# Three attention units in flight, and four gate products of branch C around the norm of branch A

## The reference

```
# block 1, mixing part (per layer)
y_mla = causal_mla_attention(...) @ w_o_mla          # 8 heads, 96 wide
y_hg  = hgrn2_branch(...) @ w_o_hg
y_mem = memory_branch(...) @ w_o_mem                 # 4 heads, 128 wide
merged = gates[0] * y_mla + gates[1] * y_hg + gates[2] * y_mem
x = x + merged @ w_out

# block 2, mixing part (per layer)
ya = diff_attention(...)        # A: 4 heads, softmax(q0 k0) - lam * softmax(q1 k1), then an rms norm
yb = nsa_attention(...)         # B: 8 heads, three softmaxes each (compressed, selected, window)
yc = swa_sink_attention(...)    # C: 8 heads, window of 128 with a sink
merged = sigmoid(ga) * (ya @ w_branch[0]) + sigmoid(gb) * (yb @ w_branch[1]) + sigmoid(gc) * (yc @ w_branch[2])
h = h + merged @ w_out
```

## Time and profile before

| | before |
|---|---|
| median of three runs | 3007.83 us |
| lowest and highest | 3001.94 and 3012.53 us |
| the profiled execution's own time | 3003.04 us |
| its span | 3001.3 us |
| mean granted TensorE clock | 0.983 of full |
| TensorE matmuls busy | 2910.9 us, 97% |
| TensorE weight loads busy | 2741.8 us, 91% |
| VectorE busy | 1695.5 us, 56% |
| ScalarE busy | 1188.8 us, 40% |
| DMA | 474.41 MB, mean 158 GB/s |

### The profile page before, as it was taken

The page is one execution under the profiler, slowest core; times in us unless marked ns, Lnnn a source line. Parts: engine busy times, 40 slices in busy tenths (PEclk is TensorE's granted clock), DMA queues, the critical chain, the costliest instruction groups (busy, mean ns, idle before and its releaser), DMA issues.

```text
span 3001.3 us, 49531 instructions
## 1 busy us (share of the span) xinstructions
PE 2910.9 (97%) x21376; PEld 2741.8 (91%) x21376; DVE 1695.5 (56%) x2824; ACT 1188.8 (40%) x1771; POOL 12.6 (0%) x20
## 2 busy tenths in 40 slices
PE   8999999999998999999999998999989999899998
PEld 8998788999998878899999996789989999678998
DVE  5666543665666553466666444456656654454665
ACT  5535422444445432244444233234454432332444
POOL 0000000000000000000000000000000000000000
PEclk9999999999999999999999898999999999999999
DMA  7544385555544344455664642445545565234553
GB/s 246 177 152 123 111 205 168 169 179 186 183 158 148 100 140 154 154 183 176 193 200 155 184 129 71 108 163 183 182 156 183 172 181 143 85 99 148 183 182 110
DMA packets 481273, 474.41 MB, mean 158 GB/s; under 512 B 47104, under 2 KB 464416, under 8 KB 480928
## 3 DMA queue, kind: packets, MB, share of 16 engines
q1 hardware_dynamic: 477472, 460.75, 49.2%
q0 software_dynamic: 3584, 10.49, 1.6%
HBM read 464.91 MB, written 6.29 MB: 157 GB/s over the span
## 4 chain that ended last, share of the span: by engine, by line
PE 92%; DVE 4%; ACT 3%; issue 1%; DMA 0%; DVEq 0%; ACTq 0%; SPq 0%
PE ps L829 33%; PE ps L928 32%; PE ps L949 17%; PE ps L982 4%; PE ps L1052 2%; PE ps L1022 1%; DVE WL L1676 1%; ACT WH L1349 1%; PE ps L872 1%; PE ps L876 1%; PE ps L880 1%; ACT REGION L1318 0%; PE ps L860 0%; DVE REGION L1819 0%; ACT L1335 0%
## 5 line engine op out<-in xcount | busy, mean ns | idle before, releaser
L1676 DVE TENSOR_TENSOR WL<-RAW,WH 128x2048 fp32r<-128x2048 f32 (+1 forms) x350 | 780.5, 2235 | 483.7 <-ACT WH L1349 481.6
L1349 ACT ACTIVATE WH<-RAW 128x2048 fp32r<-128x2048 f32 (+1 forms) x350 | 647.2, 1860 | 138.1 <-DMA RAW<-in_w_in 53.8
L949 PE MATMUL ps<-HH,WL 128*128 128x256 f32 x1408 | 394.8, 280 | 0.0
L949 PE MATMUL ps<-HH,WH 128*128 128x256 f32 x1408 | 394.3, 280 | 0.0
L949 PE MATMUL ps<-HL,WH 128*128 128x256 f32 x1408 | 394.0, 280 | 0.0
L928 PE MATMUL ps<-UH,WH 128*128 128x256 f32 x2688 | 378.5, 283 | 0.5 <-DVE WL L1676 0.5
L928 PE MATMUL ps<-UH,WL 128*128 128x256 f32 x2688 | 377.3, 283 | 0.0
L928 PE MATMUL ps<-UL,WH 128*128 128x256 f32 x2688 | 376.4, 282 | 0.0
L928 PEld LDWEIGHTS ps<-UH,WH 128*128 128x128 f32 x2688 | 346.2, 190 | 1.1 <-DVE WL L1676 0.7
L928 PEld LDWEIGHTS ps<-UL,WH 128*128 128x128 f32 x2688 | 346.7, 191 | 0.0
L928 PEld LDWEIGHTS ps<-UH,WL 128*128 128x128 f32 x2688 | 346.2, 190 | 0.0
(11 more groups left out here) (269 smaller groups left out, 3159.9 us busy)
## 6 DMA issues: line engine op xcount, KB each, us to landing
RAW<-in_w_ffn_in SPq DMA_DIRECT2D x88, 1024.0 KB, 5.1
RAW<-in_ffn_wi SPq DMA_DIRECT2D x88, 1024.0 KB, 5.1
RAW<-in_w_in SPq DMA_DIRECT2D x86, 1024.0 KB, 5.3
RAW<-in_w_ffn_out SPq DMA_DIRECT2D x32, 1024.0 KB, 5.1
RAW<-in_ffn_wo SPq DMA_DIRECT2D x32, 1024.0 KB, 5.2
RAW<-in_w_out SPq DMA_DIRECT2D x16, 1024.0 KB, 5.2
RAW<-in_w_ffn_out SPq DMA_DIRECT2D x16, 768.0 KB, 4.5
RAW<-in_ffn_wo SPq DMA_DIRECT2D x16, 768.0 KB, 4.5
```

The lines of the kernel that those rows point to most:

```text
L949: last = nc.tensor.matmul(bank(n + side, 0, T), a[:, k, side * P:(side + 1) * P], b[:, k0 + k, :], start=k0 + k == 0 and a is wh and b is ...
L1349: nc.scalar.activation(split_ap(s, part_high(s)), raw_ap(s), ACT.Copy).then_inc(weights_high, 1)
L1676: v_.tensor_tensor(split_ap(s, part_low(s)), raw_ap(s), split_ap(s, part_high(s)).bitcast(FP), ALU.subtract)\
```

## The change

- `S` gets a third place per kind (i % 3), and so do the maxima and sums; `PT` keeps two. The new helper `sums` gives the place; B's small compressed probabilities get an array `CS` of their own, so that `S` doesn't grow.
- TensorE issues scores(i+3) instead of scores(i+2) in step i; the scores of units 0, 1 and 2 come ahead of step 0. Gate product 0 comes between the scores of units 1 and 2, in `B` between those of units 0 and 1. The transposes of the last unit move one step up, right behind those of the last unit but one and ahead of the last gate product.
- ScalarE does the exponentials of units 0 and 1 first, then per step: tanh of gate(i), copy of transposes(i), exponentials(i+2).
- VectorE does the scores of units 0 and 1 first, then per step: scaling(i), scores(i+2), output(i-1).
- Four (`EARLY`) of C's eight gate products move: one between A's attention and the sums of squares of A's norm, three between these and A's out-projection. Two slabs of weights move with them. Their tanh comes after the norm on ScalarE, and they are kept in arrays that are free then (`SILU`, `V`, `RSTD`) until C's outputs are merged. C's attention keeps four gate products, in units 0, 2, 4 and 6.

The core of the diff (where `S[:, b, par, ...]` is only replaced by `sums(kind, i, b, ...)`, and for helpers of the numbering on the other engines, it is left out):

```diff
+EARLY = 4
+def gate_tiles(kind, unit):
+    if kind == "C":
+        return [EARLY + unit // 2] if unit % 2 == 0 else []
+    n = DK // ATTN[kind][0]
+    return range(unit * n, (unit + 1) * n)
+def transposed(kind, step):
+    last = ATTN[kind][0] - 1
+    return [] if step < 0 or step == last else [step, last] if step == last - 1 else [step]
+def gated_unit(kind, step):
+    if step < 0:
+        return 0 if step == (-3 if kind == "B" else -2) else None
+    return step + 1 if step + 1 < ATTN[kind][0] else None
...
-    for i in range(-2, units):
-        if i >= 0:
+    for step in range(-3, units):
+        for i in transposed(kind, step):
             t[i] = n
             n += n_t
-        if i + 2 < units:
-            s[i + 2] = n
+        if step + 3 < units:
+            s[step + 3] = n
             n += n_s
-        if 0 <= i + 1 < units:
-            f[i + 1] = n
-            n += n_f
-        if i >= 0:
-            o[i] = n
+        unit = gated_unit(kind, step)
+        for m in gate_tiles(kind, unit) if unit is not None else []:
+            f[m] = n
+            n += 1
+        if step >= 0:
+            o[step] = n
             n += 1
...
         attention(L + "A", "A")
+        pl.products(L + "C.early0", 1)
         pl.products(L + "A.norm", 2)
+        pl.slab_first[L + "C.early"] = len(pl.slab_last)
+        pl.products(L + "C.early1", EARLY - 1)
+        for m in range(0, EARLY - 1, 2):
+            pl.slab(pl.first[L + "C.early1"] + m)
         pl.slabs(L + "A.out", [4, 4])
...
-        MX = sb("MX", [P, 2, 3, 2])
-        SUM = sb("SUM", [P, 2, 3, 2])
+        MX = sb("MX", [P, 3, 3, 2])
+        SUM = sb("SUM", [P, 3, 3, 2])
...
+        def sums(kind, i, b, keys):
+            if kind == "B":
+                return CS[:, i % 3, :, keys] if b == 0 else S[:, i % 3, b - 1, :, keys]
+            return S[:, i % 3, 0, :, keys]
+        def early_gate(m):
+            return SILU[:, m, :] if m < 2 else V[:] if m == 2 else RSTD[:]
...
# TensorE, block 2
+                early_product(first[L + "C.early0"], slab_first[L + "C.early"], 0)
                 pe.wait_ge(squares_ready, tally.add("squares_ready") + 1)
                 for i in range(2):
                     n = first[L + "A.norm"] + i
                     product(n, [(bank(n), [(ones, AQ[:, 2 * i:2 * i + 2, :])])])
+                for m in range(1, EARLY):
+                    early_product(first[L + "C.early1"] + m - 1, slab_first[L + "C.early"] + m // 2, m)
...
# ScalarE, attention
+                exponentials(0)
+                exponentials(1)
+                for i in range(units):
+                    if i < units - 1:
+                        gates(i)
+                    turned(i)
+                    if i + 2 < units:
+                        exponentials(i + 2)
+                gates(units - 1)
...
# ScalarE, block 2
                 norm(TMP[:], TMP[:])
+                for m in range(EARLY):
+                    n = first[L + "C.early1"] + m - 1 if m else first[L + "C.early0"]
+                    half_tanh(n, early_gate(m), bank(n, 0, T))
                 attention(L + "B", "B", merged=L + "A.out")
...
# VectorE, attention
-                        if i >= 2:
-                            wait_product(dve, t[i - 2] + b)
+                        if i >= 3:
+                            wait_product(dve, t[i - 3] + b)
...
                 scores(0)
+                scores(1)
                 for i in range(units):
-                    if i + 1 < units:
-                        scores(i + 1)
                     scale_probs(i)
+                    if i + 2 < units:
+                        scores(i + 2)
                     if i >= 1:
                         outputs(i - 1)
```

More of the change, by code:

```diff
@@ L325, in attention @@
         pl.slab_first[name] = len(pl.slab_last)
-        for m in range(1, DK, 2):
-            pl.slab(f[m * ATTN[kind][0] // DK] + m % (DK // ATTN[kind][0]), split=kind == "mem", places=places)
+        for m in range(EARLY + 1 if kind == "C" else 1, DK, 2):
+            pl.slab(f[m], split=kind == "mem", places=places)
         pl.products(name, n)
@@ L999, in tokens, with early_product @@
                 product(n, [(o, [(act[:, k, tt * P:(tt + 1) * P], wk(k)) for k in range(kt)]) for o, wk, tt in parts])
+            def early_product(n, s, m):
+                wait_weights(pe, s)
+                product(n, [(bank(n, 0, T), [(slot(s, DK, 256)[:, k, m % 2 * P:(m % 2 + 1) * P], U[:, k, :]) for k in range(DK)])])
             def attention(name, kind, scores, values):
@@ L1006, in attention @@
                 base = tally.add("probs_ready", units)
-                for i in range(-2, units):
-                    if i >= 0:
+                for step in range(-3, units):
+                    for i in transposed(kind, step):
                         pe.wait_ge(probs_ready, base + i + 1)
-                        qt, par = i % 2, i % 2
+                        qt = i % 2
                         for b in range(n_t):
@@ L1023, in attention @@
                             last.then_inc(product_done, 1)
-                    if i + 2 < units:
-                        for b, groups in enumerate(scores(i + 2)):
+                    if step + 3 < units:
+                        for b, groups in enumerate(scores(step + 3)):
                             if n_s == n_b:
-                                n = s[i + 2] + b
+                                n = s[step + 3] + b
                                 product(n, [(bank(n)[:, g * T:g * T + k.shape[-1]], [(q, k)]) for g, (q, k) in enumerate(groups)])
@@ new lines, in exponentials @@
+                def exponentials(i):
+                    act.wait_ge(max_ready, base + i + 1)
+                    for b in range(n_b):
+                        cmp = kind == "B" and b == 0
+                        nk = blocks(i % 2) if cmp else T if kind == "mem" else (i % 2 + 1) * P
+                        nk += kind == "C"
+                        for g in range(2):
+                            dst = sums(kind, i, b, slice(0, nk))[:, g]
+                            src = bank(s[i])[:, g * T:(g + 1) * T] if kind == "mem" else dst
+                            last = nc.scalar.activation(dst, src, ACT.Exp, bias=MX[:, i % 3, b, g:g + 1],
+                                                        scale=scale, accum_out=SUM[:, i % 3, b, g:g + 1])
+                    last.then_inc(evicted[s[i] % BANKS] if kind == "mem" else exp_done, 1)
@@ new lines, in turned @@
+                def turned(i):
+                    if i >= 2:
+                        wait_product(act, o[i - 2])
+                    for b in range(n_t):
+                        cmp = kind == "B" and b == 0
+                        keys = 1 if cmp else NT if kind == "mem" else i % 2 + 1
+                        c = (1 if kind == "A" else 2) * keys * P
+                        rows = slice(0, blocks(i % 2)) if cmp else slice(0, P)
+                        evict(t[i] + b, PT[rows, b, i % 2, 0:c], bank(t[i] + b)[rows, 0:c])
@@ new lines, in gates @@
+                def gates(i):
+                    if kind == "mem":
+                        feed.to(slab_first[name] + min(3, i + 2))
+                    for m in gate_tiles(kind, i):
+                        half_tanh(f[m], GATE[:, m, :], bank(f[m], 0, T))
+                exponentials(0)
[6 more added lines that the diff above has]
+                        exponentials(i + 2)
```

76 lines of the change are left out of this document (26 added, 50 removed).

## The result

The changed kernel takes **2973.75 us** (median of five, 2971.67 to 2977.85), the kernel before, run beside it, 3002.65 (2996.52 to 3012.53): 28.9 us less, ratio 0.991, 95% interval 0.9894 to 0.9926, 22 to 32 us. 2995.4 was forecast, with 2984 as the lower end: the sign was right, the size was not. Of the 21.7 us between forecast and result 5.2 are the base, since the forecast stood on a median of three runs of before (3007.83) and five give 3002.65; the other 16.5 are the change.

A forecast was written before the change was run, and what follows sets the result against it. TensorE, busy for 97% of the span, was taken as the bound, so only its gaps and clock could be won. 24.5 - 4.9 - 0.4 - 6.8 = 12.4 us less than 3007.83 gave 2995.4 us, range 2984 to 3007.

The forecast's parts named there:

- Point 1: Around A's norm: four of C's gate products fill TensorE's wait and avoid half clock; 24.5 us saved over both layers.
- Point 2: Last unit's transposes, moved ahead of the last gate, wait for VectorE's scaling in attention stages; 4.9 us lost.
- Point 3: First units of C and A: small waits of unit 1's transposes against waits newly hidden; 0.4 us lost.
- Point 4: B's start: unit 2's scores wait 5.9 us for a PSUM bank until ScalarE reads the gate; 6.8 us lost.
- Point 5: Middle of B and C: units without a gate and bank reuse cost nothing; 0, ends 0 and -7 us.
- The rival of a C bound by the round trip: C's units without a gate wait for the chain through ScalarE and VectorE; slower, 3014 us, chance 0.1.
- The sum: All parts of the change together: 24.5 - 4.9 - 0.4 - 6.8 = 12.4 us less.
- the waits cost clock as well: Rival: B's start loses 12 us, two other places with waits lose 1.7 each; 3.8 us gained, 3004, chance 0.25.

The follow-up runs named there:

- b_shift64: Kernel before with only MX and SUM enlarged from two places to three, every instruction the same: 2986.6 us, 2999.6 for before beside it.
- a_no_early: Changed kernel without the four early gate products, C doing all eight itself, three units in flight kept: 2998.9 us, 2999.8 for before beside it.
- a_plast: Changed kernel with VectorE scaling the last unit's exponentials ahead of an earlier unit's output copy: 2967.7 us, 3001.8 for before beside it.
- a_gate_late: Changed kernel with B's first gate product issued behind the scores of unit 2 instead of unit 0: 2968.6 us, 2999.8 for before beside it.
- a_two_deep: Changed kernel back to two units in flight in all three engines' orders, early gates kept: 2988.9 us, 2999.8 for before beside it.
- a_oldaddr: Changed kernel with MX and SUM at the end of memory, region and weights at before's addresses: 2995.4 us, 2999.6 for before beside it.
- a_again: Changed kernel run once more, unaltered: 2976.0 us, 2999.8 for before beside it.
- a_tanh_first: Changed kernel with ScalarE reading B's first gate product before the exponentials of unit 1: 2977.9 us, 3001.8 for before beside it.
- a_places: Changed kernel with pads so all six feed-forward weight places start at a multiple of 128 bytes: 2984.1 us, 2999.6 for before beside it.

## Why the prediction missed

- **Part by part.** The failed step is in the list of parts itself: MX and SUM grow from two places to three, and I costed that at nothing without a word. It moves all of REGION by 64 bytes. By b_shift64 it is worth 12.9 us between the medians. 12.4 + 12.9 = 25.3 of the 28.9; the 3.6 left are less than executions of one kernel differ, and the better clock of after's executions is worth more than that. "In the middle of every attention stage there is no idle time ... the change is worth what it does at A's norm, at the last unit and at the first" holds for the order of the work, and I took it for all. The range was built from the same list, on the high base, and so held no case above 24 us.
- **Point 1, four early gates.** Right. From V(7), the last four of the six matmuls at 1789.76, so 0.22 later, to the out-projection at 1805.96 it is 15.98 us, for 16.6; no wait, and clock 1.00 over 1794 to 1826. By a_no_early 22.5 us for 24.5. What I left unsaid: it is worth that only with three units in flight, and nothing with two.
- **Point 2, T(last).** Right, its cause too. T(last) waits 0.76, 0.80, 1.50, 1.37 and 0.76 us in mla, mem, A, B and C, and K(7) of C 0.38, where K(last) had cost 7.4 in all ten stages: 11.2 in both layers, 3.8 more, for the 4.9 of the sum. a_plast takes it away by moving P(last).
- **Point 3, first units.** T(1) of C waits 0.53 and 0.66: small, as said.
- **Point 4, B's start.** The wait is 5.89 for 5.9, by the mechanism given. The clock cost more than I had: half of 8.17 and of 5.34 busy us, 6.8 in both layers, for the 5.0 taken; against that stand the 3.4 given back. In time, what a_gate_late wins back is 8 us, beside the 6.8 that I had the point cost. The T(0) that was to come 12.4 us behind S(0) (2600.21 to 2612.6) came 13.46 behind it.
- **Point 5, middle.** 0, right: the stretch of C above has no bracket. The rival of a C bound by the round trip is out for after, and is just what happens in a_two_deep.
- **The sum.** In the trace it holds. From A's first scores to C's out-projection, where points 1 to 5 lie but for mla and mem, the stretches of TensorE are (us, layers 0 and 1):

| stretch | before | after | less in both layers (minus: more) | by the forecast's terms |
|---|---|---|---|---|
| A's first scores to V(7) | 37.3, 37.6 | 38.1, 38.1 | -1.3 | -1.6 |
| V(7) to the end of A's out-projection | 28.0, 28.4 | 29.9, 29.9 | -3.4 | -4.7 |
| B | 72.4, 69.1 | 75.9, 74.5 | -8.8 | -7.8 |
| C | 42.8, 42.4 | 28.9, 28.9 | 27.4 | 27.0 |
| all | | | 13.9 | 12.9 |

In a_oldaddr, without the shift, the same stretches are 15.4 us less than in before. By time the program without the shift is worth 7 us (4 to 11) by a_oldaddr and about 12 by a_again against b_shift64. The first interval leaves 12.4 out by 2, and just takes in the 3.8 of the rival *the waits cost clock as well*; but the trace of after has no half clock at all at A's end and in C, where that rival had 3.4 us of its loss (in a_again and a_tanh_first C's out-projection has some), and B lost 8.8 us and not the 13 of that rival. What a_oldaddr's time lacks lies outside them, in part in things that the sum has nowhere: the six waits for VectorE's split of the weights (`WL`) are 10.2 us in place of 8.7, and half clock costs 34 us outside these stretches (half of TensorE's busy time at a granted clock of 0.50), in before 31. Whether the second goes with the program or with the execution isn't shown.

## What to carry to other kernels

An edit that makes a tile larger moves all that is allocated behind it; where TensorE is busy for 97% of the time, write down the address of both operands modulo 128 bytes before and after, and run the old kernel with the new sizes alone before any gain is put down to the new order. Try a pad: here 64 bytes between the addresses of weights and activations were worth more than the whole change of order. And where steps are moved past each other on one engine, number the PSUM banks and look what else the engine's queue holds ahead of the step: both losses of this change were of that kind, could be read from the trace of before, and went away with a few lines.

## What was not expected of the hardware

- The spacing of fp32r matmuls of 128 x 256 at full clock goes with the distance of the two operands' addresses in a partition: in the first feed-forward products 113.3 ns at 64 bytes modulo 128 in most stages, 116.7 to 120.0 otherwise. In the second ones it is 117.8 at 64 and 118.2 at 32.
- It can differ between stages of one execution with equal operands and places: 117.3, 118.7 and 120.0 in a_places.
- Two executions of the same instructions (before and b_shift64) had a mean granted clock of 0.98 and 0.95 in the same stage, and the second took 6 us longer for it.
